# Two-layer kernel: 32 more tokens leave the dense up projection, and the pair search looks at 112 of 256 sums

## What is computed

```python
q = _rms((xt @ w_q).reshape(T, P_HEADS, P_KEY_DIM))            # 8 heads
s1 = einsum('thd,hnd->thn', q[..., :half], sub_keys[:, 0])      # 128 keys
s2 = einsum('thd,hnd->thn', q[..., half:], sub_keys[:, 1])
v1, i1 = top_k(s1, 16)
v2, i2 = top_k(s2, 16)
cand = (v1[..., :, None] + v2[..., None, :])                    # 16 x 16 sums
vals, ci = top_k(cand, 16)
e = i1[ci // 16] * 128 + i2[ci % 16]        # 8 x 16 = 128 experts of a token
g = softmax(vals)
a = einsum('cd,ckd->ck', xc, expert_u[ec])  # up projection
w = g * gelu(a)
y = einsum('ck,ckd->cd', w, expert_v[ec])   # down projection
```

## Time and profile before

| | us |
|---|---|
| median of three runs | 2269.31 (2267.72 to 2269.32) |
| the profiled execution's own time | 2267.63 |
| its span, first to last instruction | 2266.0 |
| PE busy | 2211.8 (98%) |
| DVE busy | 1559.9 (69%) |
| ACT busy | 1075.8 (47%) |
| POOL busy | 445.4 (20%) |

### The profile page before, as it was taken

The page is one execution under the profiler, slowest core; times in us unless marked ns, Lnnn a source line. Parts: engine busy times, 40 slices in busy tenths (PEclk is TensorE's granted clock), DMA queues, the critical chain, the costliest instruction groups (busy, mean ns, idle before and its releaser), DMA issues.

```text
span 2266.0 us, 34831 instructions
## 1 busy us (share of the span) xinstructions
PE 2211.8 (98%) x12445; PEld 1970.3 (87%) x12445; DVE 1559.9 (69%) x3128; ACT 1075.8 (47%) x1963; POOL 445.4 (20%) x355
## 2 busy tenths in 40 slices
PE   7999999999999888899999999999999999999999
PEld 5888888888878446678999999999999999999999
DVE  4444444433376787443588898999987888888886
ACT  5344344322244577533444345888883333333332
POOL 0000000000030000010000100655544344444440
PEclk9999999999999999999999999999999999999999
DMA  4232223223244100032455765999999999999993
GB/s 170 93 94 91 83 83 99 77 93 111 83 159 127 47 1 1 1 100 96 123 165 155 230 189 164 355 409 386 391 384 365 398 374 376 382 380 377 379 386 121
DMA packets 129632, 458.95 MB, mean 203 GB/s; under 512 B 13936, under 2 KB 30320, under 8 KB 127584
## 3 DMA queue, kind: packets, MB, share of 16 engines
q1 hardware_dynamic: 74592, 232.29, 30.5%
q0 software_dynamic: 51312, 195.58, 22.8%
q10 hardware_dynamic: 3600, 29.36, 3.3%
HBM read 405.80 MB, written 50.86 MB: 202 GB/s over the span
## 4 chain that ended last, share of the span: by engine, by line
PE 95%; ACT 2%; DVE 2%; issue 0%; DMA 0%; POOL 0%; ACTq 0%; PEldq 0%; DVEq 0%; POOLq 0%
PE bank L442 19%; PE bank L443 19%; PE bank L444 19%; PE bank L1161 8%; PE bank L1163 8%; PE bank L1162 8%; PE bank L1133 4%; PE bank L457 2%; PE bank L557 1%; PE bank L517 1%; PE bank L735 1%; PE bank L754 1%; PE bank L772 1%; ACT pair_prob L1387 1%; PE bank L1102 1%; ACT pair_prob L1293 1%
## 5 line engine op out<-in xcount | busy, mean ns | idle before, releaser
L442 PE MATMUL bank<-act_hi,whi 128*128 128x384 f32 (+1 forms) x1968 | 721.7, 367 | 7.6 <-DVE act_lo L1645 6.4
L443 PE MATMUL bank<-act_lo,whi 128*128 128x384 f32 (+1 forms) x1968 | 711.2, 361 | 0.0
L444 PE MATMUL bank<-act_hi,wlo 128*128 128x384 f32 (+1 forms) x1968 | 711.0, 361 | 0.0
L429 DVE TENSOR_TENSOR wlo<-raw,whi 128x1024 fp32r<-128x1024 f32 x398 | 485.6, 1225 | 316.3 <-ACT whi L425 314.5
L425 ACT ACTIVATE whi<-raw 128x1024 fp32r<-128x1024 f32 x398 | 418.5, 1056 | 394.8 <-PE bank L1163 331.1
L442 PEld LDWEIGHTS bank<-act_hi,whi 128*128 128x128 f32 x1968 | 370.5, 188 | 52.9 <-issue 16.5
L444 PEld LDWEIGHTS bank<-act_hi,wlo 128*128 128x128 f32 x1968 | 370.1, 188 | 37.8
L443 PEld LDWEIGHTS bank<-act_lo,whi 128*128 128x128 f32 x1968 | 370.6, 188 | 36.0 <-issue 0.5
L1161 PE MATMUL bank<-h_hi,whi 128*128 128x384 f32 x1024 | 342.1, 334 | 1.8 <-issue 1.8
L1162 PE MATMUL bank<-h_lo,whi 128*128 128x384 f32 x1024 | 342.0, 334 | 0.0
L1163 PE MATMUL bank<-h_hi,wlo 128*128 128x384 f32 x1024 | 342.0, 334 | 0.0
(11 more groups left out here) (358 smaller groups left out, 2452.5 us busy)
## 6 DMA issues: line engine op xcount, KB each, us to landing
raw<-tiles SPq DMA_DIRECT2D x398, 512.0 KB, 4.4
gates_dram<-stage ACTq DMA_DIRECT2D x12, 2048.0 KB, 10.2
wg<-gates_dram POOLq DMA_DIRECT2D x16, 1536.0 KB, 13.4
acts_dram<-gelu SPq DMA_DIRECT2D x120, 192.0 KB, 4.5
hf<-acts_dram POOLq DMA_DIRECT2D x30, 768.0 KB, 9.3
bias<-alibi POOLq DMA_DIRECT2D x16, 256.0 KB, 2.8
w1s<-cmp_w POOLq DMA_DIRECT2D x1, 4096.0 KB, 13.8
res<-x_t ACTq DMA_DIRECT2D x4, 512.0 KB, 6.1
```

The costliest lines, as they stand in the source:

```text
L429: dve.tensor_tensor(wlo[:, j.slot, :], raw[:, j.slot, :], whi[:, j.slot, :].bitcast(F32), ALU.subtract).then_inc(lo_made, 1)
L442: pe.matmul(to, wh, x, start=(kc == 0), stop=False)
L443: pe.matmul(to, wh, xl, start=False, stop=False)
L444: last = pe.matmul(to, wl, x, start=False, stop=(kc == KC - 1))
```

## The change

The names `EXTRA` = 32 and `FIRST` = 160 come in. Tokens 128 to 159 leave the dense up projection: U jobs run on 352 columns. Their U rows are fetched instead: 32 tokens by 128 experts are 32 fetches of 128 rows (table "x" in `USES`; partition 32s+i holds token i's experts 32s to 32s+31), and 32 more dots against `xtok_extra`, which PE builds by four products of each chunk into four groups of 32 partitions. The gelu of these dots is multiplied into the tokens' gate weights (`weigh_extra`), and the dense gelu is set to 1 in their columns, so that the down projection stays at 384 columns. Their gates are made last. The search of pairs takes only places (a, b) with a < 4, or b < 4: 64 + 48 = 112 sums in place of 256, with new arithmetic for the place. The U jobs per tile are 13, 13, 18 and 24, and dots begin in the third tile: 13 there, 27 in the fourth, 80 in the first 44 turns of the gates, 12 in the rest. So the dots before the down projection are 132, and with V rows 156 uses are left for it. In the last four turns of the gates DVE makes all weighted one-hots.

```diff
-U_TILE = 17
-U_GATES = U_FIRST + TT * U_TILE
+EXTRA = 32
+FIRST = P + EXTRA
+TILE_JOBS = [13, 13, 18, 24]
+TILE_AT = [U_FIRST + sum(TILE_JOBS[:tt]) for tt in range(TT)]
+U_GATES = U_FIRST + sum(TILE_JOBS)
...
+EXTRA_Q = (DT - EXTRA) // 8
...
-DOTS_GATES = 2
-DOTS_REST = 1
-SEEN_GATES = DOTS_GATES * DT // 8
-SEEN_U = SEEN_GATES + DOTS_REST * (P - U_REST)
+DOTS_TILE = [(0, 0), (0, 0), (13, 6), (27, 0)]
+DOTS_GATES = 80
+DOTS_REST = 12
+SEEN_GATES = sum(n for n, _ in DOTS_TILE) + DOTS_GATES
+SEEN_U = SEEN_GATES + DOTS_REST
+OWN_AHEAD = 40
+
+U_USES = [("u", n) for n in range(OWN_AHEAD)] + [("x", n) for n in range(EXTRA)] + [("u", n) for n in range(OWN_AHEAD, P)]
...
-            pool.wait_ge(S("idx_made"), 1)
+            pool.wait_ge(S("idx_made"), 5)
...
-                x = turn(pe, bank[5 + kc // 4][:, (kc % 4) * P:(kc % 4 + 1) * P], hg[:, kc, 0:P], ident)
+                cols_ = slice((kc % 4) * P, (kc % 4 + 1) * P)
+                turn(pe, bank[5 + kc // 4][:, cols_], hg[:, kc, 0:P], ident)
+                for s in range(4):
+                    x = pe.matmul(bank[(4, 7)[kc // 4]][32 * s:32 * s + EXTRA, cols_], hg[:, kc, P:FIRST], ident,
+                                  start=True, stop=True)
...
-                multiply(pe, Job(J_U + n), act_hi, act_lo, first=P)
+                multiply(pe, Job(J_U + n), act_hi, act_lo, first=FIRST)
...
-                def beside(m):
-
-                    u_job(U_FIRST + U_TILE * tt + m)
+                def beside(at_):
+
+                    for m in range(tile_job(tt, at_), tile_job(tt, at_ + 1)):
+                        u_job(TILE_AT[tt] + m)
+                    n, first_at = DOTS_TILE[tt]
+                    for _ in range(n * max(0, at_ - first_at) // (17 - first_at), n * max(0, at_ + 1 - first_at) // (17 - first_at)):
+                        use_row()
...
-                then(dve.tensor_tensor(cand[:, :, :, :], vv[:, :, 0, :].unsqueeze(3).broadcast_to((P, 8, 16, 16)),
-                                       vv[:, :, 1, :].unsqueeze(2).broadcast_to((P, 8, 16, 16)), ALU.add))
+                for a0, a1, n_b, at_, next_ in ((0, 4, 16, 0, mark), (4, 16, 4, 64, then)):
+                    n_a = a1 - a0
+                    next_(dve.tensor_tensor(
+                        cand[:, :, at_:at_ + n_a * n_b].rearrange("p h (a b) -> p h a b", a=n_a),
+                        vv[:, :, 0, a0:a1].unsqueeze(3).broadcast_to((P, 8, n_a, n_b)),
+                        vv[:, :, 1, 0:n_b].unsqueeze(2).broadcast_to((P, 8, n_a, n_b)), ALU.add))
...
-                then(dve.tensor_scalar(ca[:, 1, :, :], vci[:, :, :], 15, None, ALU.bitwise_and))
-                then(dve.tensor_copy(caf[:, :, :, :], ca[:, :, :, :]))
+                mark(dve.tensor_scalar(ca[:, 1, :, :], vci[:, :, :], 2, None, ALU.logical_shift_right))
+                then(dve.tensor_copy(spot[:, :, :], vci[:, :, :]))
+                then(dve.tensor_copy(shifted[:, :, :, :], ca[:, :, :, :]))
+                then(dve.scalar_tensor_tensor(out=caf[:, 0, :, :], in0=shifted[:, 1, :, :], scalar=-12.0,
+                                              in1=shifted[:, 0, :, :], op0=ALU.add, op1=ALU.max))
+                then(dve.tensor_scalar(shifted[:, 0, :, :], caf[:, 0, :, :], -4.0, -48.0, ALU.mult, ALU.add))
+                then(dve.scalar_tensor_tensor(out=shifted[:, 1, :, :], in0=caf[:, 0, :, :], scalar=-16.0,
+                                              in1=shifted[:, 0, :, :], op0=ALU.mult, op1=ALU.max))
+                then(dve.tensor_tensor(caf[:, 1, :, :], shifted[:, 1, :, :], spot[:, :, :], ALU.add))
...
+                    for s in range(4):
+                        dve.tensor_copy(idx_extra[32 * s:32 * s + 32, :], idxf[0:EXTRA, 32 * s:32 * s + 32])\
+                            .then_inc(S("idx_made"), 1)
...
-                for _ in range(DOTS_GATES):
-                    use_row(seen)
-                    seen += 1
-            for n in range(U_REST, P):
-                make_lo(dve, Job(J_U + n).ahead())
-                for _ in range(DOTS_REST):
-                    use_row(seen)
-                    seen += 1
+                if q < EXTRA_Q:
+                    for _ in range(DOTS_GATES * q // EXTRA_Q, DOTS_GATES * (q + 1) // EXTRA_Q):
+                        use_row()
+            for n in range(KEPT):
+                make_lo(dve, Job(J_U + U_REST + n).ahead())
+                if n == 2:
+                    dve.wait_ge(S("gates_made4"), 4 + DT // 4)
+                    dve.memset(hf[:, 0, :, 0:EXTRA], 1.0).then_inc(S("extra_step"), 1)
+                for _ in range(DOTS_REST * n // KEPT, DOTS_REST * (n + 1) // KEPT):
+                    use_row()
+            dve.wait_ge(S("extra_step"), 6)
```

More of the change, by code:

```diff
@@ L84, in used_by, with tile_job, gate_tokens @@
     return SEEN_U + min(V_USES, V_USES * (jj + 1) // V_LAST)
-ALL_DOTTED = next(jj for jj in range(P) if used_by(jj) >= 2 * P - SEEN_U) + 1
+ALL_DOTTED = next(jj for jj in range(P) if used_by(jj) >= SEEN_U + 2 * U_LATE) + 1
+def tile_job(tt, m):
+    return m * TILE_JOBS[tt] // 17
+def gate_tokens(gi):
+    return (4 * gi + EXTRA) % DT
 AHEAD = 2
@@ L722, in _ @@
                     load_gates((four + 3) // 2)
-                while n < 2 * P and four_of_use(n - ROWS) == four:
+                while n < len(USES) and four_of_use(n - ROWS) == four:
                     gather(n)
@@ L1091, in _ @@
             u_job(1)
[L1092 removed]
+            pe.wait_ge(S("x_step"), 7)
             for b in range(2):
@@ L1502, in _ @@
             for h in range(2):
+                copy(xtok_extra[:, 4 * h:4 * h + 4, :], bank[(4, 7)[h]][:, :].rearrange("p (k d) -> p k d", k=4),
+                     S("x_step"))
+            for h in range(2):
                 copy(xtok[:, 4 * h:4 * h + 4, :], bank[5 + h][:, :].rearrange("p (k d) -> p k d", k=4), S("x_step"))
+            act.wait_ge(S("extra_step"), 1)
             act.wait_ge(ssq_made, 3)
@@ L2121, in _ @@
             add_halves(7)
+            dve.wait_ge(S("halves_added"), 8)
+            dve.memset(gelu[:, :, 0:EXTRA], 1.0).then_inc(S("extra_step"), 1)
             u_job(0)
@@ L2273, in _ @@
                     dve.wait_ge(S("gates_made4"), gi + 1)
-                    t, slot = 4 * gi, gi % 4 * 4
-                    for x in range(2):
+                    t, slot = gate_tokens(gi), gi % 4 * 4
+                    for x in range(2 if q < EXTRA_Q else 4):
                         dve.tensor_scalar(hot[:, slot + x, 1, :], iota, selT[:, 1, t + x:t + x + 1],
```

130 lines of the change are left out of this document (81 added, 49 removed).

## The result

The changed kernel takes 2273.44 us, the median of 11 runs (2269.16 to 2283.38), against 2268.92 for the kernel before in as many: a ratio of 1.0031, with a 95% interval of 1.0016 to 1.0047. It is slower by 0.31%, where the forecast was 2268.6 and no change. Its runs form two groups with nothing between: six from 2269.2 to 2273.4 and five from 2279.1 to 2283.4. The kernel before shows one group in these comparisons, 3 us wide. The profiled execution took 2279.1 us (span 2277.0) and is of the upper group. So everything read from it is 5.7 us above the median, and the sum can only be judged beside a second trace, of the lower group (e0).

A forecast was written before the change was run, and what follows sets the result against it. PE was taken to bound selection, gates and down projection, DVE the selection after the change. +2.6 - 1.3 + 1.7 - 15.4 + 10.7 + 1.0 + 0 = -0.7 us on 2267.63, 2266.9; median 1.7 above: 2268.6, range 2256 to 2279.

The forecast's parts named there:

- stage 0: Before the selection: 32 more products on PE in its first two query jobs, +2.6 us, between +1.5 and +6.8.
- U jobs 0 to 3: Before the selection: four narrower up-projection jobs on PE, 0.32 us less each, -1.3 us.
- selection: The bound changes from PE to DVE, which waits 12.7 us: 297.7 us against 296.0, +1.7.
- gates: PE stays the bound; 48 turns go from 5.95 to 5.63 us, -15.4 us, to -12 if DVE loses its lead.
- seam: Between gates and down projection: DVE must use row 131 before weighing the first input; 46.9 us for 36.2, +10.7.
- clock, down projection: After the seam's wait PE runs partly at 1.2 GHz, +1.0 us (0 to 2); down projection 0, at most +1.5.
- the narrower job at a slope of 0.417 ns a column: PE's up-projection jobs: 32 columns fewer save 13.3 ns a matmul, 0.32 us a job, 41 us for 128 jobs.
- rival 5: Up-projection matmuls: width does nothing, a floor at 173 ns; gates keep 5.95 us, +16, 2284 us; chance 0.02.
- rival 1: Selection: DVE less of a bound, stage toward 287.4 us, -8.6 instead of +1.7, in all 2258; chance 0.24.
- rival 3: Selection: DVE's own work dearer; at 2 us a tile more, +7.3 us over the run before, 2277; chance 0.24.
- Rival 4: Selection: PE granted 1.2 GHz around its waits, high parts later too, +5 to +15 us, 2280; chance 0.04.
- Rival 2: Between gates and down projection: row wait covered, 33.6 us there, -13.3 instead of +10.7, 2244 to 2250; chance 0.07.

The follow-up runs named there:

- e0: The changed kernel once more, unaltered, for a second trace: 2268.18 us, ratio 1.0009.
- e1: The changed kernel with the up projection's matmuls back on 384 columns, the 32 extra columns computed and not used: 2291.38 us, ratio 1.0100.
- e5: The changed kernel with 8 dots in the rest, 12 instead of 40 in the selection, the others beside the down projection: 2240.95 us, ratio 0.9875.
- e14: The changed kernel with each of POOL's first 13 fetches issued only when the one before has landed: 2290.38 us, ratio 1.0100.
- e3: The kernel before with only the pair search changed, to 112 of 256 sums: 2268.64 us, ratio 1.0000.
- e12: The changed kernel with the gelu's store issued ahead of the weight load on SP: 2270.51 us, ratio 1.0012.
- e4: The changed kernel with 8 dots in the rest in place of 12, the four others beside the down projection: 2263.61 us, ratio 0.9962.
- e8: The changed kernel with its U matmuls on 368 columns, the 16 more computed and not read: 2280.32 us, ratio 1.0054.

## Why the prediction was wrong

The steps against the two profiled executions of the same kernel, in us, each as a difference to the kernel before:

| step | forecast | upper group | lower group (e0) |
|---|---|---|---|
| stage 0 | +2.6 | +4.4 | +4.4 |
| U jobs 0 to 3 | -1.3 | -1.5 | -1.5 |
| selection | +1.7 | +7.1 | +3.4 |
| gates | -15.4 | -7.9 | -16.9 |
| seam | +10.7 | +7.3 | +7.8 |
| clock, down projection | +1.0 | +1.6 | +2.6 |
| sum | -0.7 | +11.0 | -0.2 |

**The step that failed is the narrower job at a slope of 0.417 ns a column.** The mechanism was right, and the size is wrong: 352 columns lie outside the two measured widths, and there a job has two costs. A turn of 5.63 us was forecast; 5.59 and 5.78 were found, and so -16.9 or -7.9 us in the gates for the -15.4. The bounds that I gave for the width (nothing, or the slope) include the slow pace, but I went by the slope and gave rival 5 only its far end. A time that is one of two, 9 us apart, can't be read from one width's rows; it would have taken a row near 352.

This step explains the upper group, 5 of 11 runs in the first comparison. It does not explain all of the median: the six runs of the lower group alone have a median of 2271.8, 3.2 us over the forecast, and none of them has a trace. In e0 the lower group's is 2266.8, 1.8 us under it.

**Selection.** That DVE becomes the bound was right, and is shown by e1 (17 us more work on PE, 0.6 us more time), e5 (fewer dots shorten it) and e14 (a wait on DVE lengthens it one for one). Its own work was right: busy 281.4 and 282.5 us for 280.6, and e3 has the search to 0.1 us. So neither rival 1 (the stage toward 287.4) nor rival 3 (dearer own work) occurred. Mis-sized are the waits. For DVE 12.7 us were worked out, 2.3 of them for a row; it waits 15.1 us in e0 and 17.6 in the upper profile for high parts (the 8.6 us just ahead of the stage taken off), and for no row. That is +2.4 and +4.9 us, and the stage is 1.7 and 5.4 over the forecast. e12 excludes the order of the stores as the cause, e1 PE's speed. The rest stays open. In two of the profiles, the upper one and e12's, one gelu in the third tile starts 4 us late and DVE then waits 5.7 and 6.5 us for the high part behind it; in e0 it does not. But e12's stage is 299.8 us all the same, so that wait isn't what makes the upper profile's 303.1: e0, e4, e8 and e12 have 299.3 to 300.2, the upper profile and e1 303.1 and 303.7.

**Rival 4 occurred, at a small price.** PE's waits grew to 2.2 and 2.5 us, and with these two the clock fell to 1.2 GHz. The first drop in the upper profile:

```profile
1221.10:1224.50 3.40, 3.14 (x11) 3.14 (x12) 3.37 (x3) 0.00 (x0) 0.00 (x0) 0.51 0.41 124
```

In 3.4 us at half speed PE loses 1.7 us, so the two drops cost at most some 3.5 us, not the 5 to 15 of the rival. No experiment takes them alone away; that DVE, which is the bound, absorbs part of it is argued from e1 and e8, which have no such drop and whose stages (303.7 and 300.2 us) are not shorter than e0's with its drops (299.4). The Trainium skill, "TensorE: Matmul & The Clock Gate", Part 1, has the low clock as the default that only activity lifts; the trace agrees with it. The selections of e0, e4, e5 and e12 have such drops too, and my chance of 0.04 was too low for that.

**Gates.** The rest of the step held: PE is busy all but 1.2 us of the stage, DVE 262.5 of 269.6 us, and the transfers did not stop it. In e0 they ran at 382 GB/s for 269.6 us. That is 103.0 MB, loads and stores together, where 99.7 were forecast. In e5's down projection, where 99% of the bytes are loads, they ran at 390 GB/s for 535.6 us. So the rule that transfers from HBM are held to about 358 GB/s (the Trainium skill, "DMA: Bandwidth & Descriptors", section "Where 436 GB/s comes from") does not hold for this kernel, which runs on one core alone: by it the gates with their 103.0 MB would have taken 288 us. That the slow pace gives almost the 278 us that the prediction worked out by this rule is chance: PE is busy in 277.45 of the 278.60 us of the upper profile.

**Seam.** The mechanism was right in each part, and e4 shows it. 13.5 + 8.7 + 20.9 us up to the last row were forecast; in e0 it is 11.05 (1694.55 less the stage's end) + 6.55 + 21.4. From there to PE's start it is 5.0 us for 3.8, since two dots follow and not one. 44.0 us in all, for 46.9. Rival 2, in which this wait is covered, is excluded: DVE waits 14.2 us there. In and after it the clock was low for 10 us in the upper profile and 14 in e0, and PE worked in only the last 4 and 6 of these: +1.6 and +2.6 us in the down projection for +1.0, and e4, without the wait, has none of it.

**Stage 0.** Chunks of the query job, before and after (starts of the transposes, and of the new products):

```profile
1003.22 0.27 PE L457 MATMUL bank<-con,hg 128*128 128x128 f32 x1
1003.25 0.47 PE L442 MATMUL bank<-act_hi,whi 128*128 128x512 f32 x1
...
1004.72 0.27 PE L457 MATMUL bank<-con,hg 128*128 128x128 f32 x1
```

```profile
1004.28 0.27 PE L484 MATMUL bank<-con,hg 128*128 128x128 f32 x1
1004.48 0.43 PE L1107 MATMUL bank<-con,hg 128*32 128x128 f32 x8
1004.83 0.50 PE L469 MATMUL bank<-act_hi,whi 128*128 128x512 f32 x1
...
1006.33 0.27 PE L484 MATMUL bank<-con,hg 128*128 128x128 f32 x1
```

1.50 us a chunk became 2.05: 0.55 for the 0.36 worked out, eight times, +4.4 for +2.6. The products overlap as in the earlier trace rows (eight records, 0.35 us to the next matmul). But what follows the transpose now starts 0.20 us after it and not 0.03, a cost of each chunk that I had not counted.

**The chances.** The sum for the lower group is right within 0.5 us, and e0's median, 2268.18, lies 0.4 us from the forecast. That is luck: it was the sum of errors, -1.5 in the gates and -2.9 in the seam against +1.8, +1.7 and +1.6 elsewhere. In the upper group nothing makes up for the 7.5 us missing in the gates. Of one kernel, then, one comparison gives +0.31% and the other no change. The median of the first is the uppermost run of its lower group, and it hangs on how many runs fall into each. Open is also why both groups lie 5 us lower in the second comparison (e0) than in the first, with the kernel before unchanged. The selection could be part of it (303.1 us in the first profile, 299.4 in e0), but with one trace of each that isn't shown.

## What to carry to other kernels

A slope of matmul time over width holds only between widths that the trace shows; before a plan rests on a new width, measure it in more than one run, and look at the distance of the starts. When work moves from a full engine to one that is 90% busy, move it to the stage where that engine has room: the same 28 dots cost 12.7 us in the selection and nothing in the down projection. And before a count in a stage is raised, find where its last fetch stands in the queue: four dots too many cost 11 to 12 us here.

## What was unexpected of the hardware

- At 352 columns matmuls in f32r start 158.3 or 166.7 ns apart at the full clock, by the job; at 360 columns 163.7 or 166.7, at 344 160.0, at 368 166.7. So 344 is slower than 352 can be.
- The pace holds within a job and mostly over many, and changes only where other work, a wait or a stretch at the low clock has come between: 47 of 48 gate jobs of one execution were slow and none of another, with the same program.
- What follows a transpose starts 0.20 us after it if it is a product on 32 columns of weights, and 0.03 after it if it is a matmul of 512 columns.
- Transfers averaged 382 GB/s over 270 us (e0, gates), 390 over 536 us (e5, down projection), and 413 over 8 us.
